# The front of a hybrid attention and pooling step, rebuilt without a transposed copy of x

## The chip, the cores and the metric

One NeuronCore of a Trainium2 chip runs the whole step. The metric is the device time of one execution in microseconds (us), as the median of some runs.

## What is computed

One layer works on 1024 prompt tokens and 8 sequences of 16 new tokens, 1152 tokens of 1024 channels, in fp32. Each of the 9 sequences has a conditioning vector c that sets shift and scale. The part at issue is the front:

```python
def _front(x, c, pos, w_ada, b_ada, w_in):
    mod = jax.nn.silu(c) @ w_ada + b_ada
    shift, scale, gate = jnp.split(mod, 3, axis=-1)
    h = (_layer_norm(x) * (1.0 + scale[:, None, :]) + shift[:, None, :])
    proj = h @ w_in
    q, k, v, g_attn, u, g_pool = jnp.split(proj, cuts, axis=-1)
    ...
```

Behind it come windowed attention with sinks (8 query heads, 2 key heads), a pooling mixer of four windows, SiLU gates, an output projection and a layer norm of alpha*x + gate*y.

## The kernel before

The kernel is written with an order by hand: each engine has its own program, and semaphores join them. An engine never passes a waiting instruction of its own.

**Units.** The input projection is cut into units: a block of 128 output columns (kinds k, v, ga, q, u, gp) for a chunk c of 384 tokens (chunks 0, 1, 2; chunk 2 has 256 prompt tokens and the 128 sample tokens). Units 0 to 5 are (k,0), (v,0), (k,1), (v,1), (k,2), (v,2). Products are made from a high and a low part, each operand as hi + lo with hi the value rounded to fp32r: per channel tile k (8 tiles of 128 channels) three matmuls, w_hi·h_hi, w_hi·h_lo, w_lo·h_hi, of 384 columns each, 24 a unit. Behind unit 5 the units 6 and up, attention slots among them, and the output projection fill TensorE's queue.

**The front.** SyncE loads x by tiles of 128 tokens (xs, a ring of XS = 6 tiles), the adaptive weights w_ada in six pieces of 512 columns (ada 0 to 3 shift and scale, in the order ADA = [0, 2, 1, 3, 4, 5], so that pieces 0 and 1 give shift and scale of channels 0 to 511; 4 and 5 the gate) and w_in by blocks. For each tile of x DVE makes statistics (x_stats, L969), GpSimd the inverse deviation (inv_std, L1260), ScalarE normalises in place (normalise, L786), TensorE transposes (x_transpose, L533, two halves of four channel tiles into the two PSUM banks of t_ps), and DVE and ScalarE copy these into xnT (evac_xt, L977 and L797), a copy of x with channels on partitions. For a piece of w_ada: ada (L505, TensorE, into s_ps), evac_ada (L790, ScalarE, into part), select (L525, TensorE, into o_ps), modulation (L981, DVE, into shT and s1T). Then h_ops (L992, DVE) applies scale and shift to xnT in place, h_high (L805, ScalarE) rounds to h_hi, and h_low (L1016 DVE, L1273 GpSimd) subtracts for h_lo, by pairs of channel tiles (H_ORDER). The samples of chunk 2 are modulated by h_samples (L1007). w_high (ScalarE) and w_low (DVE for blocks 0 and 1, GpSimd for the rest) do the same for w_in.

TensorE runs the first four units by halves (low: channel tiles 0 to 3; high: 4 to 7) with the transposes and the adaptive pieces between. Unit 3 has bank 0 of s_ps (EARLY), the others share three banks of proj_ps:

```python
            select(0)
            select(1)
            unit(0, low)
            x_transpose(3)
            unit(1, low)
            ...
            unit(3, low)
            for n in range(4):
                unit(n, high)
```

## Time and profile before

| | us |
|---|---|
| median of 3 runs | 462.62 |
| their range | 462.58 to 463.11 |
| the profiled execution | 464.38 |
| its span | 462.6 |
| TensorE matmul busy in the span | 429.2 (93%) |
| DVE busy | 285.5 (62%) |
| ScalarE busy | 129.9 (28%) |
| GpSimd busy | 118.4 (26%) |

PE is TensorE, DVE VectorE, ACT ScalarE, POOL GpSimd. The busy time of PE holds overlaps of pipelined matmuls, so it is not work at the peak rate. The mean granted clock of TensorE is 0.986 of full speed (2.4 GHz). In a row of a timeline, the bracket at the end is the idle time in front of the instruction and what ended it.

### The profile page before, as it was taken

How to read it: one execution, taken by the hardware profiler on the slowest of the kernel's cores; microseconds unless marked ns; L12 is line 12 of the kernel's file. 1: busy time of each engine (PE TensorE's matmuls, PEld its weight loads, DVE VectorE, ACT ScalarE, POOL GpSimd, SP SyncE). 2: the span in 40 equal slices, each digit the busy share in tenths (PEclk: the TensorE clock that was granted, in tenths of full speed). 3: DMA queues.
4: the chain of work that ended last, by engine and by line, in shares of the span. 5: the costliest groups of instructions: out<-in, count | busy, mean ns of one | idle time of the engine just before them, and what ended most of it. 6: DMA issues, size and time to landing. Idle time of an engine off the chain costs nothing.

```text
span 462.6 us, 6622 instructions
## 1 busy us (share of the span) xinstructions
PE 429.2 (93%) x2598; PEld 370.6 (80%) x2598; DVE 285.5 (62%) x541; ACT 129.9 (28%) x307; POOL 118.4 (26%) x83
## 2 busy tenths in 40 slices
...
GB/s 303 416 419 326 228 0 1 123 106 170 160 15 33 136 47 45 52 6 47 53 2 14 43 47 7 47 51 2 179 49 53 92 91 91 92 91 92 91 116 67
DMA packets 22545, 46.30 MB, mean 100 GB/s; under 512 B 11089, under 2 KB 13649, under 8 KB 21202
## 3 DMA queue, kind: packets, MB, share of 16 engines
...
q8 instruction: 21, 0.34, 0.3%
q14 instruction: 10, 0.08, 0.1%
...
## 4 chain that ended last, share of the span: by engine, by line
PE 78%; DVE 12%; ACT 4%; issue 3%; DMA 2%; POOL 1%; SPq 0%; DVEq 0%; POOLq 0%
PE proj_ps L585 14%; PE proj_ps L587 14%; PE proj_ps L586 14%; PE proj_ps L718 7%; PE proj_ps L720 7%; PE proj_ps L719 7%; PE t_ps L541 2%; PE s_ps L618 2%; PE t_ps L647 2%; PE s_ps L521 2%; DMA xs<-x_all 2%; DVE wo_lo L1143 2%; DVE xnT L1001 1%; ACT Pb L868 1%; PE proj_ps L561 1%
## 5 line engine op out<-in xcount | busy, mean ns | idle before, releaser
L585 PE MATMUL proj_ps<-h_hi,w_hi 128*128 128x384 f32 x400 | 139.2, 348 | 0.3 <-DVE rt L1036 0.3
L587 PE MATMUL proj_ps<-h_hi,w_lo 128*128 128x384 f32 x400 | 135.2, 338 | 0.0
L586 PE MATMUL proj_ps<-h_lo,w_hi 128*128 128x384 f32 x400 | 135.1, 338 | 0.0
L1271 POOL TENSOR_TENSOR w_lo<-w_raw,w_hi 128x1024 fp32r<-128x1024 f32 x16 | 41.4, 2585 | 154.1 <-ACT w_hi L814 154.1
L585 PEld LDWEIGHTS proj_ps<-h_hi,w_hi 128*128 128x128 f32 x400 | 75.8, 189 | 4.9 <-issue 2.2
L586 PEld LDWEIGHTS proj_ps<-h_lo,w_hi 128*128 128x128 f32 x400 | 75.8, 189 | 0.9
L587 PEld LDWEIGHTS proj_ps<-h_hi,w_lo 128*128 128x128 f32 x400 | 75.6, 189 | 0.0
L718 PE MATMUL proj_ps<-wo_hi,m_hi 128*128 128x512 f32 (+1 forms) x152 | 58.9, 387 | 4.4 <-DVE wo_lo L1143 3.8
L719 PE MATMUL proj_ps<-wo_lo,m_hi 128*128 128x512 f32 (+1 forms) x152 | 58.4, 384 | 0.0
L720 PE MATMUL proj_ps<-wo_hi,m_lo 128*128 128x512 f32 (+1 forms) x152 | 58.4, 384 | 0.0
L1058 DVE SCALAR_TENSOR_TENSOR mixed<-th,proj_ps 128x384 f32<-128x384 f32 x24 | 13.3, 553 | 56.5 <-ACT th L828 56.5
L718 PEld LDWEIGHTS proj_ps<-wo_hi,m_hi 128*128 128x128 f32 x152 | 28.6, 188 | 11.8 <-issue 4.3
L720 PEld LDWEIGHTS proj_ps<-wo_hi,m_lo 128*128 128x128 f32 x152 | 28.6, 188 | 6.2
L1263 POOL TENSOR_TENSOR rstd<-veps,mhalf 128x1 f32<-128x1 f32 x18 | 10.6, 589 | 89.8 <-DVE veps L967 89.8
L719 PEld LDWEIGHTS proj_ps<-wo_lo,m_hi 128*128 128x128 f32 x152 | 28.6, 188 | 6.0
L814 ACT ACTIVATE w_hi<-w_raw 128x1024 fp32r<-128x1024 f32 x18 | 18.9, 1057 | 38.3 <-PE proj_ps L587 33.9
L828 ACT ACTIVATE th<-proj_ps 128x384 f32<-128x384 f32 x24 | 11.8, 492 | 59.9 <-PE proj_ps L587 59.9
L868 ACT ACTIVATE Pb<-s_ps,negm 128x192 f32<-128x192 f32 (+3 forms) x72 | 28.1, 400 | 0.0
L881 ACT ACTIVATE m_hi<-mixed 128x1024 fp32r<-128x1024 f32 x9 | 9.5, 1059 | 62.5 <-PE proj_ps L720 61.7
L1246 DVE SCALAR_TENSOR_TENSOR yr<-yr,rstd,lnB 128x1024 f32<-128x1024 f32 (+1 forms) x10 | 25.8, 2590 | 0.3
L1136 DVE TENSOR_TENSOR den<-rs,es 128x4 f32<-128x4 f32 (+1 forms) x20 | 5.2, 259 | 33.5 <-ACT Pb L868 33.5
L1334 POOL TENSOR_TENSOR m_lo<-mixed,m_hi 128x1024 fp32r<-128x1024 f32 x8 | 23.5, 2935 | 4.1 <-ACT m_hi L881 4.1
...
## 6 DMA issues: line engine op xcount, KB each, us to landing
...
```

Of the source, the lines that this page charges most:

```text
L585: pe.matmul(bank[:, 0:CW], w_hi[:, w, k, :], hi, start=(k == 0), stop=False)
L586: pe.matmul(bank[:, 0:CW], w_hi[:, w, k, :], lo, start=False, stop=False)
L587: mm = pe.matmul(bank[:, 0:CW], w_lo[:, w, k, :], hi, start=False, stop=(k == KT - 1))
L718: pe.matmul(o, m_hi[:, t % 2, k, :], wo_hi[:, k, w], start=(k == 0), stop=False)
L719: pe.matmul(o, m_hi[:, t % 2, k, :], wo_lo[:, k, w], start=False, stop=False)
L720: mm = pe.matmul(o, m_lo[:, t % 2, k, :], wo_hi[:, k, w], start=False, stop=(k == KT - 1))
L814: act.activation(w_hi[:, b % 2], w_raw[:, b % RAW], ACT.Copy).then_inc(whi_done, 1)
L868: e = act.activation(Pb[:, i % 2, j, 0:nk], src, ACT.Exp, bias=negm[:, i % 2, j:j + 1], scale=SCALE, accum_out=rs[:, i % 2, j:j + 1])
L1058: dve.scalar_tensor_tensor(dst, th[:, i % 2, :], 1.0, src, ALU.add, ALU.mult).then_inc(dve_free, 1)
L1246: dve.scalar_tensor_tensor(r[:, w], r[:, w], rstd[:, TILES + t:TILES + t + 1], lnB[:, w], ALU.mult, ALU.add).then_inc(yb_done, 1)
L1271: pool.tensor_tensor(w_lo[:, b % 2], w_raw[:, b % RAW], w_hi[:, b % 2].bitcast(F32), ALU.subtract).then_inc(wlo_done, 1)
L1334: pool.tensor_tensor(m_lo[:, (t + 1) % 2], mixed[:, :, P * (t + 1):P * (t + 2)], m_hi[:, (t + 1) % 2].bitcast(F32), ALU.subtract).then_inc ...
```

## The change

xnT goes. xs now holds all nine tiles of x and lies where xnT lay (that room later takes mixed). The unit of work of the front is a channel tile of one chunk, listed in T_ORDER: first channel tiles 0 to 3 of chunks 0 and 1, then 4 and 5 of both, 6 and 7 of both, then chunk 2, where the samples come as two pieces ("s", four channel tiles each). TensorE transposes a channel tile of a chunk (three, two or for samples four transposes) into one of two banks of t_ps; DVE's h_full multiplies and adds from PSUM into a ring hx of HX = 5 places; ScalarE's h_high rounds hx into h_hi; GpSimd's h_low alone makes every low part of the prompt, and then the hx place is free. The bank of t_ps is free after h_full of it.

w_ada's columns are permuted on the host: piece a (0 to 3) holds shift and scale of the channel pair 2a, 2a+1. All four go through bank 1 of s_ps, so ada(a) waits until part a-1 is copied. Unit 2 has bank 0 of s_ps. x tiles 0 to 2 are loaded ahead of all adaptive weights, tiles 3 to 5 behind the first two pieces, 6 to 8 behind the last. TensorE's first six units run in pieces (first_unit), each with transposes of later tiles woven in. DVE makes w_lo of block 2 as well (DVE_LOW = 3).

```diff
-ADA = [0, 2, 1, 3, 4, 5]
-XS = 6
+HX = 5
...
+T_ORDER = [("p", c, k) for c in range(2) for k in range(4)] + [("p", c, k) for a in (4, 6) for c in range(2) for k in (a, a + 1)]
+T_ORDER += [("s", 2, 0)] + [("p", 2, k) for k in range(4)] + [("s", 2, 1)] + [("p", 2, k) for k in range(4, KT)]
+HI_ORDER = T_ORDER[:16] + [T_ORDER[m] for m in (17, 16, 18, 19, 20, 22, 21, 23, 24, 25)]
+LOW_ORDER = [x for x in T_ORDER if x[0] == "p"]
+SPARE_UNIT = 2
+BANK_BEFORE = {5: 3, 6: 0}
+DVE_LOW = 3
...
SyncE
-            load_ada(0)
             load_x(0)
+            load_x(1)
+            load_x(2)
...
-            load_ada(1)
+            load_ada(0)
             load_w(0)
             load_w(1)
+            load_ada(1)
             load_x(3)
             load_x(4)
             load_x(5)
+            load_ada(2)
+            load_ada(3)
             load_x(6)
             load_x(7)
             load_x(8)
...
-            sp.wait_ge(xt_done, 2 * TILES)
-            sp.dma_start(wada_late[:], w_ada[ADA[4]]).then_inc(ld_late, 16)
+            sp.wait_ge(ada_done, 4)
+            sp.dma_start(wada_late[:], w_ada[4]).then_inc(ld_late, 16)
...
TensorE
+            def x_transpose(*taus):
+                for tau in taus:
+                    kind, c, k = T_ORDER[tau]
+                    b = tau % 2
...
+                    if tau >= 2:
+                        pe.wait_ge(hx_done, tau - 1)
...
+            def first_unit(n, slices, taus=()):
...
+                for k in slices:
+                    if c == 2 and k % 4 == 0:
+                        pe.wait_ge(hhi_done, hi_count(("s", 2, k // 4)))
+                    pe.wait_ge(hhi_done, hi_count(("p", c, k)))
+                    pe.matmul(bank[:, 0:CW], w_hi[:, w, k, :], h_hi[:, k, cols(c)], start=(k == 0), stop=False)
+                    pe.matmul(bank[:, 0:CW], w_lo[:, w, k, :], h_hi[:, k, cols(c)], start=False, stop=False)
+                    if taus:
+                        x_transpose(taus.pop(0))
+                for k in slices:
+                    pe.wait_ge(hlo_p, LOW_ORDER.index(("p", c, k)) + 1)
...
+                    mm = pe.matmul(bank[:, 0:CW], w_hi[:, w, k, :], h_lo[:, k, cols(c)], start=False, stop=(k == KT - 1))
...
+            x_transpose(0, 1)
             ada(0)
...
             select(0)
+            first_unit(0, (0, 1), (2, 3))
+            first_unit(1, (0, 1))
+            ada(1)
             select(1)
+            first_unit(0, (2, 3))
+            first_unit(1, (2, 3))
             ada(2)
+            x_transpose(4, 5)
             select(2)
+            first_unit(2, (0, 1, 2, 3), (6, 7))
+            ada(3)
+            first_unit(3, (0, 1), (8, 9))
             select(3)
+            first_unit(3, (2, 3))
+            first_unit(0, (4, 5), (10,))
+            first_unit(1, (4, 5), (11,))
+            first_unit(2, (4, 5), (12,))
+            first_unit(3, (4, 5), (13,))
+            first_unit(0, (6, 7), (14,))
...
+            first_unit(3, (6, 7), (17,))
+            x_transpose(18)
+            first_unit(4, range(KT), range(19, len(T_ORDER)))
+            first_unit(5, range(KT))
...
ScalarE
             normalise(0)
+            normalise(1)
+            normalise(2)
             evac_ada(0)
             w_high(0)
+            h_high(0, 1)
             w_high(1)
             evac_ada(1)
+            h_high(2, 3)
             normalise(3)
             normalise(4)
             normalise(5)
+            evac_ada(2)
+            h_high(4, 5, 6, 7)
+            evac_ada(3)
             normalise(6)
+            h_high(8, 9)
             normalise(7)
+            h_high(10)
             normalise(8)
+            h_high(11, 12, 13, 14, 15)
...
DVE
+            def h_full(*taus):
...
+                    if i >= HX:
+                        dve.wait_ge(hlo_p, i - HX + 1)
+                    dve.wait_ge(mod_done, k // 2 + 1)
+                    dve.wait_ge(xt_done, tau + 1)
+                    dve.tensor_scalar(hx[:, i % HX, 0:pw], t_ps[:, b, 0:pw], s1T[:, k, 0:1], shT[:, k, 0:1], ALU.mult, ALU.add).then_inc(hx_done, 1)
...
+            modulation(0)
             w_low(0)
+            h_full(0, 1)
             w_low(1)
+            x_stats(3)
             modulation(1)
+            h_full(2, 3)
             x_stats(4)
             x_stats(5)
+            h_full(4)
+            modulation(2)
+            h_full(5, 6, 7)
```

Two places of TensorE's queue show the move. Before, the start of the queue holds the first adaptive pieces (L521), three tiles' transposes (L541) and both selections (L530) ahead of the first projection matmul (L576):

```order
L521 MATMUL s_ps<-wada_59,cpad 32x512 x8
L541 MATMUL t_ps<-ident,xs 128x128 x16
L521 MATMUL s_ps<-wada_60,cpad 32x512 x4
L541 MATMUL t_ps<-ident,xs 128x128 x8
L521 MATMUL s_ps<-wada_60,cpad 32x512 x4
L530 MATMUL o_ps<-sel,part 128x9 x8
L576 MATMUL proj_ps<-h_hi,w_hi 128x384
L577 MATMUL proj_ps<-h_hi,w_lo 128x384
```

Now (new lines: 562 transposes, 533 adaptive piece, 542 selection, 589 and 590 the high part's two matmuls, 597 the low part's):

```order
L562 MATMUL t_ps<-ident,xs 128x128 x3
L589 MATMUL proj_ps<-h_hi,w_hi 128x384
L590 MATMUL proj_ps<-h_hi,w_lo 128x384
L562 MATMUL t_ps<-ident,xs 128x128 x3
L597 MATMUL proj_ps<-h_lo,w_hi 128x384 x2
L589 MATMUL proj_ps<-h_hi,w_hi 128x384
L590 MATMUL proj_ps<-h_hi,w_lo 128x384
L589 MATMUL proj_ps<-h_hi,w_hi 128x384
L590 MATMUL proj_ps<-h_hi,w_lo 128x384
L597 MATMUL proj_ps<-h_lo,w_hi 128x384 x2
L533 MATMUL s_ps<-wada_59,cpad 32x512 x8
L542 MATMUL o_ps<-sel,part 128x9 x4
```

The second adaptive piece (wada_59 here, wada_60 before) and its selection, which stood ahead of the first projection matmul, now stand behind two channel tiles of unit 0 and of unit 1.

Unit 4 before is one run of matmuls with no transpose in it:

```order
L577 MATMUL proj_ps<-h_hi,w_lo 128x384
L576 MATMUL proj_ps<-h_hi,w_hi 128x384
L577 MATMUL proj_ps<-h_hi,w_lo 128x384
L576 MATMUL proj_ps<-h_hi,w_hi 128x384
L577 MATMUL proj_ps<-h_hi,w_lo 128x384
L576 MATMUL proj_ps<-h_hi,w_hi 128x384
L577 MATMUL proj_ps<-h_hi,w_lo 128x384
L581 MATMUL proj_ps<-h_lo,w_hi 128x384 x8
L585 MATMUL proj_ps<-h_hi,w_hi 128x384
```

Now, from its fifth channel tile on (L562 is a transpose of the next tile):

```order
L562 MATMUL t_ps<-ident,xs 128x128 x2
L589 MATMUL proj_ps<-h_hi,w_hi 128x384
L590 MATMUL proj_ps<-h_hi,w_lo 128x384
L562 MATMUL t_ps<-ident,xs 128x128 x2
L589 MATMUL proj_ps<-h_hi,w_hi 128x384
L590 MATMUL proj_ps<-h_hi,w_lo 128x384
L562 MATMUL t_ps<-ident,xs 128x128 x2
L589 MATMUL proj_ps<-h_hi,w_hi 128x384
L590 MATMUL proj_ps<-h_hi,w_lo 128x384
L562 MATMUL t_ps<-ident,xs 128x128 x2
L589 MATMUL proj_ps<-h_hi,w_hi 128x384
L590 MATMUL proj_ps<-h_hi,w_lo 128x384
```

Each later pair of matmuls waits for hhi_done of a channel tile whose transposes stand directly ahead of it in the same queue.

## Rows read from the trace of the kernel before

**Rows 1.** Busy time by stretch: us, then each engine's busy us (instructions), clock, DMA, GB/s.

```profile
27.32:35.72 8.40, 8.00 (x34) 7.46 (x35) 8.12 (x23) 5.08 (x6) 5.26 (x9) 0.65 1.02 421
35.72:50.62 14.90, 14.56 (x113) 10.77 (x112) 10.21 (x25) 11.22 (x17) 2.09 (x6) 1.00 0.68 243
50.62:60.99 10.37, 8.74 (x50) 8.23 (x49) 10.20 (x17) 3.79 (x6) 4.34 (x3) 1.00 0.54 228
60.99:70.33 9.34, 5.09 (x26) 3.82 (x25) 9.13 (x13) 2.25 (x5) 3.29 (x2) 1.00 0.00 0
70.33:76.35 6.02, 6.02 (x26) 6.02 (x26) 4.25 (x7) 0.83 (x1) 2.44 (x1) 0.72 0.00 0
...
76.35:463.00 386.65, 373.35 (x2286) 327.50 (x2285) 229.73 (x412) 96.01 (x263) 98.47 (x55) 1.00 0.21 69
```

**Rows 2.** TensorE's timeline at the start: start us, us, line, instruction, idle before.

```profile
9.08 1.93 PE L521 MATMUL s_ps<-wada,cpad 128*32 128x512 f32 x8 [0.50 <-DMA wada<-w_ada]
14.50 3.94 PE L541 MATMUL t_ps<-ident,xs 128*128 128x128 f32 x16 [3.49 <-ACT xs L788]
...
19.94 1.09 PE L541 MATMUL t_ps<-ident,xs 128*128 128x128 f32 x8
...
24.12 1.04 PE L530 MATMUL o_ps<-sel,part 128*128 128x9 f32 x8 [1.10 <-ACT part L795]
...
27.78 0.52 PE L577 MATMUL proj_ps<-h_hi,w_lo 128*128 128x384 f32 x1
28.10 0.52 PE L576 MATMUL proj_ps<-h_hi,w_hi 128*128 128x384 f32 x1
```

**Rows 3.** TensorE's timeline later in the front.

```profile
33.64 0.34 PE L586 MATMUL proj_ps<-h_lo,w_hi 128*128 128x384 f32 x1
33.81 0.34 PE L587 MATMUL proj_ps<-h_hi,w_lo 128*128 128x384 f32 x1
...
64.72 0.44 PE L576 MATMUL proj_ps<-h_hi,w_hi 128*128 128x384 f32 x1 [2.17 <-ACT h_hi L808]
...
68.51 1.49 PE L581 MATMUL proj_ps<-h_lo,w_hi 128*128 128x384 f32 x6 [1.75 <-DVE h_lo L1020]
...
71.10 0.53 PE L585 MATMUL proj_ps<-h_hi,w_hi 128*128 128x384 f32 x1
```

**Rows 4.** GpSimd's and DVE's timeline at 64.7 us and at 250.5 us.

```profile
64.74 1.84 POOL L1277 TENSOR_TENSOR h_lo<-xnT,h_hi 128x768 fp32r<-128x768 f32 x1 [2.31 <-ACT h_hi L808]
...
64.76 2.24 DVE L1038 TENSOR_TENSOR rt<-rt,sinT 128x384 f32<-128x384 f32 x1
...
250.46 2.57 POOL L1271 TENSOR_TENSOR w_lo<-w_raw,w_hi 128x1024 fp32r<-128x1024 f32 x1 [7.29 <-ACT w_hi L814]
...
250.73 0.56 DVE L1058 SCALAR_TENSOR_TENSOR mixed<-th,proj_ps 128x384 f32<-128x384 f32 x1
```

**Rows 5.** DVE's timeline: statistics of the first two tiles of x, and a modulation.

```profile
10.41 0.69 DVE L959 BATCH_NORM_STATS2 bnst<-xs 128x6 f32<-128x512 f32 x1 [6.70 <-DMA xs<-x_all]
...
12.11 0.69 DVE L959 BATCH_NORM_STATS2 bnst<-xs 128x6 f32<-128x512 f32 x1
...
25.19 0.20 DVE L989 SCALAR_TENSOR_TENSOR s1T<-o_ps,bT 128x36 f32<-128x36 f32 x1
```

**Rows 6.** Groups of DVE instructions: xcount, busy us, mean ns, idle before.

```profile
L1001 DVE TENSOR_SCALAR xnT<-xnT,s1T,shT 128x384 f32<-128x384 f32 x16 | 8.1, 570 | 1.2 <-ACT xnT L803 1.2
...
L975 DVE TENSOR_TENSOR w_lo<-w_raw,w_hi 128x1024 fp32r<-128x1024 f32 x2 | 2.4, 1220 | 1.3 <-ACT w_hi L814 1.3
...
L1116 DVE COPY PT<-t_ps 64x256 f32<-64x256 f32 x13 | 5.4, 415 | 4.0 <-PE t_ps L647 4.0
```

**Rows 7.** Groups of ScalarE instructions.

```profile
L788 ACT ACTIVATE xs<-xs,nmr,rstd 128x1024 f32<-128x1024 f32 x9 | 11.1, 1236 | 13.6 <-POOL nmr L1266 13.6
...
L795 ACT ACTIVATE part<-s_ps 128x512 f32<-128x512 f32 x6 | 3.6, 594 | 4.6 <-PE s_ps L521 4.6
...
L840 ACT ACTIVATE uext<-proj_ps 128x256 f32<-128x256 f32 x4 | 1.5, 385 | 14.5 <-PE proj_ps L587 14.5
```

More of the change, by code:

```diff
@@ L137, with hi_count @@
 SLOTS = {PLACES[4 * s // 3]: [s] for s in range(NSTEP + 2)}
[L141 to L149 removed]
+T_ORDER = [("p", c, k) for c in range(2) for k in range(4)] + [("p", c, k) for a in (4, 6) for c in range(2) for k in (a, a + 1)]
[5 more added lines that the diff above has]
+DVE_LOW = 3
+def hi_count(x):
+    return HI_ORDER.index(x) + 1
 def keys_of(i):
@@ L316, in hybrid_step @@
     ld_late = sem("ld_late")
-    ld_x = [sem(f"ld_x{i}") for i in range(XS)]
+    ld_x = [sem(f"ld_x{i}") for i in range(TILES)]
     ld_w = [sem(f"ld_w{i}") for i in range(RAW)]
@@ L557, in unit @@
+            def unit(n):
+                kind, j, c = UNITS[n]
+                bank = unit_bank(n)
+                wait_bank(n)
                 if kind == "z":
@@ L588, in unit @@
-                if slices[-1] == KT - 1:
-                    mm.then_inc(unit_done, 1)
-            def v_transposes(m):
-                pe.wait_ge(vte_done, m - 1) if m >= 2 else pe.wait_ge(xte_hi if m else xte_lo, TILES)
+                    if n == FIRST_UNIT[b]:
+                        weights_ready(b)
+                    for k in range(KT):
+                        hi, lo = h_hi[:, k, cols(c)], h_lo[:, k, cols(c)]
+                        pe.matmul(bank[:, 0:CW], w_hi[:, w, k, :], hi, start=(k == 0), stop=False)
+                        pe.matmul(bank[:, 0:CW], w_hi[:, w, k, :], lo, start=False, stop=False)
+                        mm = pe.matmul(bank[:, 0:CW], w_lo[:, w, k, :], hi, start=False, stop=(k == KT - 1))
@@ L1016, in h_low @@
-            def h_low(c, groups):
-                for g in groups:
-                    dve.wait_ge(hhi_done, H_ORDER.index((c, g)) + 1)
-                    w = slice(2 * g, 2 * g + 2)
-                    dve.tensor_tensor(h_lo[:, w, cols(c)], xnT[:, w, cols(c)], h_hi[:, w, cols(c)].bitcast(F32), ALU.subtract).then_inc(hlo_v, 1)
+                ks = slice(2 * a, 2 * a + 2)
+                sums = o_ps[:, 0:36].rearrange("p (k s) -> p k s", s=9)
+                for m, (dst, one) in enumerate(((shT, 0.0), (s1T, 1.0))):
+                    bias = bT[:, KT * m + 2 * a:KT * m + 2 * a + 2].unsqueeze(2).to_broadcast([P, 2, 9])
+                    last = dve.scalar_tensor_tensor(dst[:, ks, :], sums[:, 2 * m:2 * m + 2, :], one, bias, ALU.add, ALU.add)
@@ L1022, in evac_unit, with samples_low @@
+            def samples_low(half):
+                dve.wait_ge(hhi_done, hi_count(("s", 2, half)))
+                ks = slice(4 * half, 4 * half + 4)
+                dve.tensor_tensor(h_lo[:, ks, SEQ:TOK], hs[:, half], h_hi[:, ks, SEQ:TOK].bitcast(F32), ALU.subtract).then_inc(hlo_v, 1)
             def evac_unit(n):
@@ L1307, in _ @@
             inv_std(2)
-            h_low(0, (0,))
+            h_low(0, 1)
             inv_std(3)
+            h_low(2, 3)
             inv_std(4)
             inv_std(5)
+            h_low(4, 5, 6, 7)
             inv_std(6)
+            h_low(8)
             inv_std(7)
+            h_low(9)
             inv_std(8)
-            h_low(0, (2,))
-            h_low(1, (2,))
-            h_low(2, (0, 2))
-            for b in range(2, NBLK):
+            h_low(*range(10, len(LOW_ORDER)))
+            for b in range(DVE_LOW, NBLK):
                 s = (b - 12) // 2 if b < NBLK - 1 else 3
```

308 lines of the change are left out of this document (126 added, 182 removed).

## The prediction

> **What bounds the kernel now.** I read the busy times by stretch first, then TensorE's timeline at the start and where it stalls (a bracket there says what ended the idle time), then the price of each kind of front instruction on the other engines.
>
> The busy times by stretch [rows 1] show two kernels in one. From 76.35 us, where the sixth projection unit (v, chunk 2) is over, TensorE is busy 373.35 of 386.65 us at granted clock 1.00: the reader should see an engine that is the bound, whatever DVE, ScalarE and GpSimd do beside it. Ahead of it is the front, with 5.09 us busy of 9.34 in one stretch and a clock of 0.65 in another. What the front gains or loses at 76.35 us I take to reach the end one to one. The question is when unit 5 ends.
>
> TensorE's timeline at the start [rows 2] shows how differently one instruction costs: 16 transposes took 3.94 us at 14.50 (246 ns each), 8 took 1.09 us at 19.94 (130 ns), the two clock levels of 1.2 and 2.4 GHz. A 128x384 matmul starts every 0.32 us on the low level (27.78 to 28.10), every 0.17 us on the high one (33.64 to 33.81, [rows 3]; 0.174 over a whole unit). The clock was high at 24.12 and low at 27.78, after gaps of 1.10 us and some 2 us; it was low again at 71.10, after gaps of 2.17 and 1.75 us [rows 3].
>
> On DVE, an instruction with two SBUF operands stands still while GpSimd works: one of 384 columns took 2.24 us beside GpSimd's 1.84 us, and one of the same width that reads PSUM took 0.56 inside a GpSimd instruction of 2.57 us [rows 4].
>
> **The change, stretch by stretch.** I follow TensorE's queue from mark to mark. T is the transposition of one channel tile of a chunk (3 transposes, 2 in chunk 2, 4 for samples); DVE turns it into hx (h_full), ScalarE into h_hi, GpSimd into h_lo. Prices: h_full of 384 columns 0.56 [rows 4], of 256 0.42 [rows 6]; h_high 0.49 and 0.39, between 0.385 for 256 and 0.594 for 512 [rows 7]; h_low 0.95 and 0.66, half and a third of 1.84 for 768 [rows 4] with a little start-up. A hand-over between engines was 0.03 us (24.12 + 1.04 to 25.19, [rows 2, 5]); I allow 0.07.
>
> *1. To the first projection matmul: 27.3 us before [rows 1], 23.5 after.* Loads run at 421 GB/s [rows 1], and 2.1 MB of w_ada was there at 9.08 us [rows 2], so the flow starts at 4.0. Tile 0 of x now is ahead of the adaptive weights: statistics start at 5.6 us, not 10.41. Three tiles at 1.70 spacing [rows 5], 10.7; GpSimd some 1.2 with hand-overs (ScalarE's total wait says no more), 11.9; normalise(2) 1.24 [rows 7], 13.1. The adaptive piece 0 (3.8 MB in all) is there at 13.2. Then on the low clock: T0, T1 6 x 0.246 = 1.5, ada(0) 2 x 1.93 = 3.9 [rows 2], part 0.6, selection 1.9 (1.04 at the high level, [rows 2]), two modulations 0.3: 21.3. w_low(0), 1.22 [rows 6], stands ahead on DVE; h_full and h_high 1.1. **3.8 us gained.**
>
> *2. To the end of the first halves of units 0 and 1: 35.72 before, 39.8 after.* Before, channel tiles 0 to 3 have their modulations by 25.4 [rows 5]. Now ada(1) stands in TensorE's queue behind two pieces of units 0 and 1, and behind ada(1) the second modulation. From 23.5: 12 matmuls x 0.32 and 6 transposes x 0.246, 28.8; ada(1) 3.9; part 0.6, selection 1.8, modulations 0.35, h_full and h_high 1.2: 36.6 for the next projection matmul. GpSimd's two h_low 1.9, 38.5; then 7 matmuls at 0.174. I take the high level from 35 us on, since only then the queue is dense. 16.3 us for 8.4: **7.9 us lost**, 4.1 behind.
>
> *3. To the end of unit 3's first half: 50.62 before, 54.3 after.* ada(2) and ada(3) 2 x 1.9, two selections 1.8, 24 matmuls x 0.174 = 4.2, T4 to T9 18 x 0.13 = 2.3, waits 2.4: 0.5 for normalise(5), which ScalarE now does behind evac_ada(1), and 1.9 in unit 2, where T6 waits until h_full(5) has freed a PSUM bank. 14.5 for 14.9. **0.4 us gained**, 3.7 behind.
>
> *4. The four second halves: 60.99 before, 68.1 after.* Before, 10.37 us without a transpose. Now 48 x 0.174 = 8.4, T10 to T17 24 x 0.125 = 3.0, waits 2.4 (normalise(8), 1.24, stands on ScalarE between h_high of two tiles; the last h_low of a pair 0.4 four times). 13.8. **3.4 us lost**, 7.1 behind.
>
> *5. Unit 4 (k, chunk 2): 70.33 before, 81.5 after.* Before 9.34 us, of which 5.09 busy. Now T18 to T25 stand one behind each channel tile's pair of matmuls, and from the fifth tile on each pair needs the T issued directly ahead of it. The round trip is 0.1 (end of T) + 0.42 + 0.39 + three hand-overs 0.2 = 1.1 us of wait, at tiles 5, 6 and 7. At tile 4 the samples' T, two DVE instructions of 512 columns (0.69 each, as those of [rows 5]) and a copy of 0.59 [rows 7] lie in it: 2.4. Tiles 0 and 2: 1.3. Waits 7.0, work 24 x 0.174 + 18 x 0.125 = 6.4. 13.4 for 9.34. **4.1 us lost**, 11.2 behind.
>
> *6. Unit 5: 76.35 before, 85.8 after.* 24 x 0.174 = 4.2 for 6.02, since ten of the old ones ran on the low clock (0.72, [rows 1]). **1.8 us gained**, 9.4 behind. w_low(2), now DVE's, stands behind two rotations of k and ends by 84.7; unit 5 hides it. Without that cover it costs up to its 1.22.
>
> Sum: -3.8 + 7.9 - 0.4 + 3.4 + 4.1 - 1.8 = **+9.4 us**.
>
> At nothing I price the later w_in blocks, cosine and sine and wada_late: all the loads of the front are some 16 MB by their sizes in the program, there by 43 us at 421 GB/s, and their users come at 78 us or later; wada_late is asked for at ada(3)'s end, near 51 us, and used behind unit 7. If those 25 us went, its 2 MB, 5 us, would show.
>
> On gaps and the clock, rows and a rule part. The rows say that gaps of 2.17 and 1.75 us within a few us were enough to lower it. The Trainium skill, "TensorE: Matmul & The Clock Gate", section "Why this matters for your kernels", asks only for gaps of no more than about 3 us; by it the clock would stay high from about 20 us on in the new front, and part 2 would take 3.5 us less, +6 in all. I go by the rows.
>
> The change also moves DVE's modulation from SBUF to PSUM. The old instruction of 384 columns took 0.57 us in the mean, standstills included [rows 6], the new one is priced at 0.56: nothing gained. The Trainium skill, "GPSIMD Engine Reference", section "Key points", names as contending with GpSimd only DVE instructions with two SBUF inputs or in a two-port mode; the row of 0.56 us inside 2.57 agrees.
>
> **Rivals.**
> *The clock stays high (chance 0.20).* For: no gap of more than 2.8 us in TensorE's new order. Against: the falls at 27.78 and 71.10. Matmuls, transposes, ada(1) and selection of part 2 up to 35 us then cost half: 3.5 us less, +6, 468.6 us; with part 1 on the high level as well another 3 less, 465.6.
> *The clock falls in unit 4 too (0.20).* Unit 4 would be busy 6.4 of 13.4 us, a smaller share than the 5.09 of 9.34 behind which it was low at 71.10. Its last 16 matmuls and unit 5's 24 on the low level: 40 x 0.15 = 6 us at most; half of it is likelier, +12.5, 475.1.
> *Faster: the round trips hide (0.08).* If DVE, ScalarE and GpSimd run ahead of TensorE, so that of the waits 2.4 + 2.4 + 7.0 none is left, unit 5 ends at 85.8 - 11.8 = 74.0, 2.3 us earlier: 460.3. For it: the first matmul is 3.8 us earlier, and DVE's standstills go. It decides where TensorE's work between a T and its user is longer than 1.1 us; in unit 4 there is none, which speaks against.
> *GpSimd becomes the bound (0.05).* All low parts of the prompt go to it, 16 x 0.95 + 8 x 0.66 = 20.5 us; from 57 us on 14 of 24 remain, 11 us of work in the 23 before unit 4's end. 0.3 more for each would still be hidden; at twice the price it would add 4: 476.
> Within 0.2%: 0.02, by chance.
>
> **The numbers.** The profiled execution has 464.38 us with a span of 462.6, 1.8 around it; it is 1.8 above the median of 462.62. The sum is made in the span, and I add it to the median: 462.6 + 9.4 = 472.0. This case (0.45) runs from 470 to 474; with the clock's two rivals the range is 465.6 to 477. What can be told from no change is 0.2%, 0.9 us. Faster 0.08, same 0.02, slower 0.90.
>
> **What would show it.** First projection matmul at 22 to 24 us; the second modulation at 33 to 36 us, the largest loss; in unit 4 gaps of over 1 us at its last tiles, released by ScalarE's h_hi; unit 5 over near 86; from there 386 us. If the second modulation is there before 30 us, or unit 4 takes less than 9, the sum is wrong; if the rest behind unit 5 is not 386 us, the step one to one is.

## The result, and the profile after

| | before | changed |
|---|---|---|
| median of 4 runs, us | 462.65 (462.58 to 463.11) | 478.25 (477.08 to 479.05) |
| ratio | 1 | 1.032, interval 1.030 to 1.034 |
| profiled execution, us (span) | 464.38 (462.6) | 478.75 (477.0) |
| granted clock over the span | 0.986 | 0.971 |

The kernel is 15.6 us slower by the medians. By the two spans it is 14.4 us; the profiled execution of before was itself 1.8 above its median, that of the changed kernel 0.5. The forecast was 472.0 us in a range of 465.6 to 477: the sign is right, the time is 1.25 us outside the range.

The marks of TensorE's queue, each read from its timeline, beside the forecast ones (us; the last column is what each piece came to minus what was forecast for it):

| mark | before | forecast | changed | forecast missed by |
|---|---|---|---|---|
| 1, first projection matmul | 27.3 | 23.5 | 20.9 | -2.6 |
| 2, end of first halves of units 0 and 1 | 35.7 | 39.8 | 36.2 | -1.0 |
| 3, end of unit 3's first half | 50.6 | 54.3 | 52.6 | +1.9 |
| 4, end of the four second halves | 61.0 | 68.1 | 67.6 | +1.2 |
| 5, end of unit 4 | 70.3 | 81.5 | 85.5 | +4.5 |
| 6, end of unit 5 | 76.35 | 85.8 | 90.55 | +0.9 |
| to the end | 386.25 more | as before | 386.45 more | +0.2 |

The view of busy times by stretch, with the changed kernel's own marks (length; then PE, PEld, DVE, ACT, POOL busy with instructions; clock; DMA; GB/s):

```profile
20.89:36.16 15.27, 12.52 (x54) 8.93 (x54) 8.01 (x20) 5.78 (x8) 6.12 (x10) 0.72 1.02 417
36.16:52.57 16.41, 15.01 (x92) 8.96 (x91) 7.08 (x18) 5.73 (x9) 6.00 (x8) 0.89 0.65 238
52.57:67.55 14.98, 13.10 (x74) 10.63 (x73) 7.89 (x17) 6.20 (x10) 8.31 (x11) 1.00 0.29 120
67.55:85.46 17.91, 10.31 (x44) 8.22 (x42) 10.47 (x21) 4.73 (x11) 6.04 (x8) 0.77 0.00 0
85.46:90.55 5.09, 5.09 (x26) 5.09 (x25) 3.85 (x7) 1.06 (x1) 0.00 (x0) 0.80 0.02 3
90.55:477.00 386.45, 373.53 (x2287) 327.66 (x2286) 229.83 (x412) 96.01 (x263) 98.51 (x55) 1.00 0.22 69
```

Against [rows 1]: from unit 6 on, next to nothing has moved (386.45 us, clock 1.00 in both). The last stretch of [rows 1] runs to 463.00, 0.4 us past the end of the span of 462.6, so what it and the prediction call 386.65 is 386.25. The whole loss stands ahead of 90.55 us, and over half of it in the fourth line, unit 4: 17.91 us where before it was 9.34. PE is busy 10.3 us there, DVE 10.5 and ScalarE 4.7. No engine is the bound; they wait for each other. The fifth line has no idle time at all but a clock of 0.80: 5.09 us for work that takes 4.16 on the high level (73.48 to 77.64 in the first experiment's timeline below).

TensorE's timeline at the start, changed kernel, as [rows 2] and [rows 3] for before (start us, length us, instruction, count, idle before it and what ended it):

```profile
17.11 1.06 PE L542 MATMUL o_ps<-sel,part 128*128 128x9 f32 x8 [0.73 <-ACT part L836]
20.89 0.66 PE L589 MATMUL proj_ps<-h_hi,w_hi 128*128 128x384 f32 x1 [2.72 <-ACT h_hi L849]
...
26.18 1.92 PE L533 MATMUL s_ps<-wada,cpad 128*32 128x512 f32 x16
28.82 1.06 PE L542 MATMUL o_ps<-sel,part 128*128 128x9 f32 x8 [0.72 <-ACT part L836]
31.50 0.44 PE L589 MATMUL proj_ps<-h_hi,w_hi 128*128 128x384 f32 x1 [1.62 <-ACT h_hi L849]
...
34.11 0.52 PE L589 MATMUL proj_ps<-h_hi,w_hi 128*128 128x384 f32 x1
34.43 0.52 PE L590 MATMUL proj_ps<-h_hi,w_lo 128*128 128x384 f32 x1
...
36.16 3.64 PE L533 MATMUL s_ps<-wada,cpad 128*32 128x512 f32 x16
```

The reader should see the two costs of the new order. Behind the first two selections the next matmul waits 2.72 and 1.62 us, a whole trip through DVE and ScalarE. And from the first projection matmul on the clock changes its level three times: the matmuls up to 26.18 us are 0.32 us apart, the low level; ada(1) takes 1.92 us for 16, the high one; those at 34.11 and 34.43 are 0.32 apart again, and ada(2) at 36.16 takes 3.57 us until the next instruction at 39.73, from where on it is high.

The same view in unit 4:

```profile
70.93 0.44 PE L589 MATMUL proj_ps<-h_hi,w_hi 128*128 128x384 f32 x1 [0.62 <-ACT h_hi L849]
...
74.99 0.44 PE L589 MATMUL proj_ps<-h_hi,w_hi 128*128 128x384 f32 x1 [2.43 <-ACT h_hi L844]
75.27 0.34 PE L590 MATMUL proj_ps<-h_hi,w_lo 128*128 128x384 f32 x1
75.44 0.38 PE L562 MATMUL t_ps<-ident,xs 128*128 128x128 f32 x2
77.01 0.53 PE L589 MATMUL proj_ps<-h_hi,w_hi 128*128 128x384 f32 x1 [1.19 <-ACT h_hi L849]
...
77.66 0.63 PE L562 MATMUL t_ps<-ident,xs 128*128 128x128 f32 x2
79.47 0.69 PE L589 MATMUL proj_ps<-h_hi,w_hi 128*128 128x384 f32 x1 [1.19 <-ACT h_hi L849]
...
82.09 0.69 PE L589 MATMUL proj_ps<-h_hi,w_hi 128*128 128x384 f32 x1 [1.18 <-ACT h_hi L849]
...
82.90 2.76 PE L597 MATMUL proj_ps<-h_lo,w_hi 128*128 128x384 f32 x8
85.46 0.52 PE L589 MATMUL proj_ps<-h_hi,w_hi 128*128 128x384 f32 x1
```

Each tile from 74.99 on has the same figure: two matmuls, T (the transposition of a channel tile), 1.19 us of nothing, the next. At the high level one round is 77.01 - 74.99 = 2.02 us, then 2.46 and 2.62. From there on the clock is low: T takes 0.63 (77.66) in place of 0.38 (75.44), and the eight last matmuls take 2.56 us where they would take 1.39. One round trip in DVE's and ScalarE's timelines:

```profile
75.96 0.54 DVE L1045 TENSOR_SCALAR hx<-t_ps,s1T,shT 128x256 f32<-128x256 f32 x1 [2.00 <-PE t_ps L562]
```

```profile
76.54 0.42 ACT L849 ACTIVATE h_hi<-hx 128x256 fp32r<-128x256 f32 x1 [1.60 <-DVE hx L1045]
```

T ends at 75.44 + 0.38 = 75.82. DVE has its result by 76.50, ScalarE from 76.54 to 76.96, the matmul starts at 77.01: 0.14 + 0.54 + 0.04 + 0.42 + 0.05 = 1.19.

### The profile page after: what moved, and what is told of

It reads as the page before. It is cut to its first block, busy times and chain, and to the rows that moved or that the text cites. A ratio compares the mean times of both kernels' runs of the same rounds, so it can differ in the third digit from the quotient of the medians.

```text
span 477.0 us, 6715 instructions
## 1 busy us (share of the span) xinstructions
PE 435.8 (91%) x2598; PEld 372.2 (78%) x2598; DVE 277.0 (58%) x535; ACT 126.9 (27%) x309; POOL 127.4 (27%) x101
## 4 chain that ended last, share of the span: by engine, by line
PE 79%; DVE 11%; ACT 4%; issue 2%; DMA 1%; POOL 1%; SPq 0%; DVEq 0%; POOLq 0%
PE proj_ps L620 13%; PE proj_ps L621 13%; PE proj_ps L622 13%; PE proj_ps L756 6%; PE proj_ps L758 6%; PE proj_ps L757 6%; PE s_ps L533 3%; PE s_ps L656 2%; PE t_ps L685 2%; DVE hx L1045 2%; PE proj_ps L589 2%; DVE wo_lo L1172 2%; PE proj_ps L597 1%; ACT Pb L909 1%; ACT h_hi L849 1%
## 5 line engine op out<-in xcount | busy, mean ns | idle before, releaser
L620 PE MATMUL proj_ps<-h_hi,w_hi 128*128 128x384 f32 x384 | 132.9, 346 | 0.0
L622 PE MATMUL proj_ps<-h_hi,w_lo 128*128 128x384 f32 x384 | 129.1, 336 | 0.0
L621 PE MATMUL proj_ps<-h_lo,w_hi 128*128 128x384 f32 x384 | 129.1, 336 | 0.0
L1293 POOL TENSOR_TENSOR w_lo<-w_raw,w_hi 128x1024 fp32r<-128x1024 f32 x15 | 38.9, 2594 | 154.5 <-ACT w_hi L855 154.5
L620 PEld LDWEIGHTS proj_ps<-h_hi,w_hi 128*128 128x128 f32 x384 | 72.2, 188 | 4.2 <-issue 2.2
L621 PEld LDWEIGHTS proj_ps<-h_lo,w_hi 128*128 128x128 f32 x384 | 72.2, 188 | 0.9
L622 PEld LDWEIGHTS proj_ps<-h_hi,w_lo 128*128 128x128 f32 x384 | 72.2, 188 | 0.0
L1303 POOL TENSOR_TENSOR h_lo<-hx,h_hi 128x384 fp32r<-128x384 f32 (+1 forms) x24 | 22.1, 924 | 41.4 <-ACT h_hi L849 25.1
L589 PE MATMUL proj_ps<-h_hi,w_hi 128*128 128x384 f32 x40 | 17.8, 446 | 12.0 <-ACT h_hi L849 8.5
L1045 DVE TENSOR_SCALAR hx<-t_ps,s1T,shT 128x384 f32<-128x384 f32 (+1 forms) x24 | 15.0, 631 | 22.3 <-PE t_ps L562 21.9
```

The source lines that it names most:

```text
L589: pe.matmul(bank[:, 0:CW], w_hi[:, w, k, :], h_hi[:, k, cols(c)], start=(k == 0), stop=False)
L620: pe.matmul(bank[:, 0:CW], w_hi[:, w, k, :], hi, start=(k == 0), stop=False)
L621: pe.matmul(bank[:, 0:CW], w_hi[:, w, k, :], lo, start=False, stop=False)
L622: mm = pe.matmul(bank[:, 0:CW], w_lo[:, w, k, :], hi, start=False, stop=(k == KT - 1))
L1045: dve.tensor_scalar(hx[:, i % HX, 0:pw], t_ps[:, b, 0:pw], s1T[:, k, 0:1], shT[:, k, 0:1], ALU.mult, ALU.add).then_inc(hx_done, 1)
L1293: pool.tensor_tensor(w_lo[:, b % 2], w_raw[:, b % RAW], w_hi[:, b % 2].bitcast(F32), ALU.subtract).then_inc(wlo_done, 1)
```

## The experiments

All edits are made to the changed kernel unless another is named. "Before" in a batch is the kernel before, run on the same chip between the others: 463.38 us in the first batch, 463.61 in the second, 463.31 in the third; ratios are to it, and are what is compared between batches (they are taken over the runs of a batch and can differ by 0.001 from the quotient of the two medians). The changed kernel was not run again in these batches: its ratio, 1.032, is that of the first table.

**Is it the round trips of unit 4?** Transposes 10 to 25 are put two to each of the eight second-half pieces, whose matmuls use older tiles, and unit 4 is left with none. The same instructions, in another order. ScalarE's order follows.

```diff
-            first_unit(0, (4, 5), (10,))
-            first_unit(1, (4, 5), (11,))
+            first_unit(0, (4, 5), (10, 11))
+            first_unit(1, (4, 5), (12, 13))
...
-            x_transpose(18)
-            first_unit(4, range(KT), range(19, len(T_ORDER)))
+            first_unit(3, (6, 7), (24, 25))
+            first_unit(4, range(KT))
```

> The changed kernel, but the transposes of chunk 2 (T18 to T25) are issued two at a time inside the eight second-half pieces of units 0 to 3, so that none is left inside unit 4. Theory A (the loss sits in unit 4's round trips, T directly ahead of its user, and in the low clock that they bring): unit 4 takes 4.2 to 4.5 us instead of 17.9, unit 5 4.2 instead of 5.1, the second halves about 1 us more; in all 12 to 14 us less than the changed kernel, 464 to 466 us. Rival B (GpSimd, which now makes all 24 low parts of the prompt, is the bound): its work of 1.0 us for 384 and 0.73 for 256 columns is the same, it waits less, but unit 4 only moves by what GpSimd runs ahead: no more than 3 us less, 475 or above. Rival C (shape of the start: the second adaptive piece in the queue): no change, 478.

Measured: 465.15 us (464.8 to 465.88), ratio 1.0037, interval 1.0022 to 1.0052. TensorE's timeline of this kernel:

```profile
62.68 0.44 PE L562 MATMUL t_ps<-ident,xs 128*128 128x128 f32 x2 [0.84 <-DVE hx L1043]
...
69.33 0.34 PE L589 MATMUL proj_ps<-h_hi,w_hi 128*128 128x384 f32 x1
...
72.10 1.55 PE L597 MATMUL proj_ps<-h_lo,w_hi 128*128 128x384 f32 x8
73.48 0.34 PE L589 MATMUL proj_ps<-h_hi,w_hi 128*128 128x384 f32 x1
...
77.64 0.34 PE L620 MATMUL proj_ps<-h_hi,w_hi 128*128 128x384 f32 x1
```

The stretch of the second halves in this kernel (columns as above):

```profile
52.74:69.33 16.59, 14.73 (x92) 12.29 (x92) 13.62 (x26) 9.40 (x18) 12.53 (x16) 1.00 0.26 108
```

Unit 4 goes from 69.33 to 73.48 without a wait, unit 5 to 77.64. The second halves take 16.59 us for the changed kernel's 14.98, since they now hold 18 transposes more. Their waits are no longer: three, for DVE to free a PSUM bank (0.84, 0.64, 0.25, together 1.7), in place of the five of the changed kernel (1.8). No matmul waits for h_hi there any more. Unit 4 then ends 12.0 us earlier. The weave takes back 13 of the 15.6 us. Theory A holds, for round trips and clock together; the next experiment parts them. GpSimd takes no less time for its 24 subtractions (22.8 us in all, for 22.0 in the changed kernel), so it was not the bound, and rival B falls; so does rival C, since the start is as it was.

**How much of unit 4 is the clock?** Five extra matmuls, whose result nothing uses, stand behind each of the last four transposes, where TensorE would be idle.

```diff
+                    if n == 4 and 3 <= k <= 6:
+                        for m in range(5):
+                            pe.matmul(s_ps[:, 1, 0:CW], w_hi[:, w, 0, :], h_hi[:, 0, cols(0)], start=True, stop=True)
```

> The changed kernel with five extra 384-column matmuls into an unused PSUM bank behind each of the transposes T22 to T25 inside unit 4; they compute nothing that is used and fill the waits of 1.2 us (5 x 0.174 = 0.87 us at the high clock). Theory A with the clock as its second half: the clock no longer falls at 77 us, tiles 5 to 7 take 2.0 us each instead of 2.6, the eight low matmuls 1.4 instead of 2.6, unit 5 4.2 instead of 5.1: 3 to 4 us less, 474 to 475.5. If gaps alone count and the clock costs nothing (rival D), the extra matmuls change nothing or cost up to 1 us: 478 to 479.

Measured: 474.94 us (473.68 to 475.5), ratio 1.0244, interval 1.0221 to 1.0268; the changed kernel's is 1.032, so 3.5 us less. Its TensorE timeline in unit 4:

```profile
74.34 0.44 PE L589 MATMUL proj_ps<-h_hi,w_hi 128*128 128x384 f32 x1 [1.55 <-ACT h_hi L847]
...
74.93 1.12 PE L595 MATMUL s_ps<-h_hi,w_hi 128*128 128x384 f32 x5
76.36 0.44 PE L589 MATMUL proj_ps<-h_hi,w_hi 128*128 128x384 f32 x1 [0.31 <-ACT h_hi L852]
...
80.40 0.44 PE L589 MATMUL proj_ps<-h_hi,w_hi 128*128 128x384 f32 x1 [0.31 <-ACT h_hi L852]
...
80.85 1.55 PE L600 MATMUL proj_ps<-h_lo,w_hi 128*128 128x384 f32 x8
82.24 0.34 PE L589 MATMUL proj_ps<-h_hi,w_hi 128*128 128x384 f32 x1
```

Its unit 4 as a stretch (clock 1.00, for 0.77 in the changed kernel):

```profile
66.91:82.24 15.33, 11.24 (x64) 9.29 (x63) 8.98 (x19) 4.72 (x11) 6.08 (x8) 1.00 0.00 1
```

Every round is now 2.02 us (74.34, 76.36, then 78.38 and 80.40), the eight last matmuls 1.39 (80.85 to 82.24), unit 5 4.16. The waits for h_hi, 0.31, are what the fill leaves of 1.19. So TensorE did more work and ended sooner, as the theory expected, and rival D falls. The clock's share is 2.6 us in unit 4 (15.33 for 17.91) and 0.9 in unit 5. Of the 13.1 us that the weave took back, 9.6 are then left for the round trips: most of them are the waits of the changed kernel's unit 4, 7.6 us, and 1.3 us of work that is slower around these.

**The place of the second adaptive product.** ada(1) and select(1) ahead of unit 1's first pieces.

```diff
             first_unit(0, (0, 1), (2, 3))
-            first_unit(1, (0, 1))
             ada(1)
             select(1)
+            first_unit(1, (0, 1))
```

> The changed kernel with one piece moved: ada(1) and select(1) ahead of unit 1's first piece on TensorE, so the second modulation does not wait for that piece. The data of ada(1) should be there by 20.5 us. Theory A says the second modulation comes 2 us earlier (28 instead of 29.9) and the mark at ada(2) 1.5 to 2.5 us earlier than 36.2; but the rest is a matter of round trips, so the end comes 0.5 to 2 us earlier, 476 to 478. Rival C (the loss is made at the start, in the order of the adaptive pieces): at least 4 us earlier, 474 or less.

Measured: 475.66 us (473.99 to 477.52), ratio 1.0263, interval 1.0226 to 1.03: some 2.6 us less, a little more than expected, and not the 4 of rival C. The wait behind select(1) falls from 1.62 to 0.48 us, and ada(2) runs at the high level (1.86 us, for 3.57). The profiled execution is the slowest of the four, and the recorded marks don't hold in it: the second selection ends at 30.4 us where the second modulation was expected at 28, and ada(2) starts 0.6 us earlier, not 1.5 to 2.5. In it 1.2 us were given away at the start (first projection matmul at 22.06, for 20.89, behind a selection at the low level, 1.88 us). At the end of unit 3's first half it is 2.3 us ahead (50.26), and in unit 4 it loses 1.3 of them again (19.25 us for 17.91), the clock being low from 68.9 us until unit 5. So the split between order and clock isn't settled by it.

**The load order at the start, both ways.** First, the changed kernel with the old load order:

```diff
+            load_ada(0)
             load_x(0)
-            load_x(1)
-            load_x(2)
...
-            load_ada(0)
+            load_x(1)
+            load_x(2)
```

> The changed kernel with the loads in the old order at the start: both halves of adaptive piece 0 ahead of x tile 0, and tiles 1 and 2 behind the small tables. First transposes then at about 14.5 us instead of 8.8, and the first projection matmul 3 to 5 us later than 20.9. Theory A: the whole queue moves back by this, 3 to 5 us more, 481 to 483, since ada(1) is behind the same instructions. If the end is set by what comes later (the loads of x tiles 3 to 8 or the adaptive pieces 2 and 3, rival E), the end hardly moves: within 1 us of 478.

Measured: 482.76 us (481.95 to 484.52), ratio 1.0421, interval 1.0396 to 1.0445. T0 is at 14.50 us in place of 8.76 and the first projection matmul at 26.88 for 20.89; some of these 6.0 are got back behind, where ada(2) takes 2.14 us for the changed kernel's 3.57. Theory A holds (481 to 483 expected). The new load order is worth 4.7 us to this kernel. Then the kernel before with the new load order:

```diff
-            load_ada(0)
             load_x(0)
+            load_x(1)
+            load_x(2)
...
-            load_x(1)
-            load_x(2)
+            load_ada(0)
```

> The kernel before with the change's load order alone: x tiles 0 to 2, the identity, the selection rows and the bias ahead of the two first adaptive weight tiles. Theory A (the load order is of use only to a kernel whose transposes come before the adaptive product; here the product still gates the modulation and the first matmul): 0 to 2 us less than the kernel before, 461 to 463. Rival F (the load order alone gives what it gave the change, 4.5 us): 458 to 459. Rival G (the product comes later, since its weights are behind the x tiles on the queue): 463.5 to 467.

Measured: 463.03 us (461.75 to 464.43), ratio 0.9991, interval 0.9978 to 1.0003: no change that can be told. Its first projection matmul is at 27.53 us, for 27.3 before. It reached the second selection 0.6 us earlier (23.52 for 24.12), and that selection then took 1.85 us, on the low level, for 1.04. The load order is worth something only to the new order of TensorE's queue: in the kernel before the first projection matmul waits for two adaptive products and the 24 transposes of three tiles of x, whichever data comes first. What the new queue order would be worth at the start without the load order was not parted from the rest.

**The price of h_full.** The shift is a constant (the line is shortened here).

```diff
-dve.tensor_scalar(hx[...], t_ps[...], s1T[:, k, 0:1], shT[:, k, 0:1], ALU.mult, ALU.add)
+dve.tensor_scalar(hx[...], t_ps[...], s1T[:, k, 0:1], 0.25, ALU.mult, ALU.add)
```

> The change with the prompt's shift replaced by the constant 0.25 in h_full: it leaves out the shift of the modulation, the number of instructions is the same. Theory P (each per-partition scalar read through a pointer costs the vector engine some 0.06 us an instruction): h_full takes 0.61 to 0.62 us for 384 tokens and 0.48 for 256 in place of 0.68 and 0.54, and the round trips of unit 4 are 0.06 us shorter each. Rival Q (it is the read from PSUM with the modulation's arithmetic that costs it): 0.68 and 0.54 unchanged. The whole time: 477 to 479 either way.

The groups of DVE instructions in the changed kernel, and then in this one (columns as in [rows 6]):

```profile
L1045 DVE TENSOR_SCALAR hx<-t_ps,s1T,shT 128x384 f32<-128x384 f32 x16 | 10.6, 674 | 15.5 <-PE t_ps L562 15.1 <-POOL h_lo L1303 0.4
...
L1045 DVE TENSOR_SCALAR hx<-t_ps,s1T,shT 128x256 f32<-128x256 f32 x8 | 4.3, 543 | 6.8 <-PE t_ps L562 6.7
```

```profile
L1045 DVE TENSOR_SCALAR hx<-t_ps,s1T 128x384 f32<-128x384 f32 x16 | 9.7, 614 | 14.1 <-PE t_ps L562 13.7 <-POOL h_lo L1303 0.4
...
L1045 DVE TENSOR_SCALAR hx<-t_ps,s1T 128x256 f32<-128x256 f32 x8 | 3.9, 482 | 7.1 <-PE t_ps L562 7.0
```

0.674 falls to 0.614 for 384 columns and 0.543 to 0.482 for 256: 0.06 us for one per-partition scalar, at both widths. Theory P holds, and each wait of 1.19 in unit 4 is 1.12. Taking 0.06 more off for the second, which wasn't run, gives an estimate of 0.554 and 0.42, the 0.56 and 0.42 that the prediction had taken from instructions without such scalars. The whole time, one run, was 475.45 us, under the 477 to 479 expected. At the end of unit 5 it is 3.3 us ahead; 2.3 of them are there at 43.2 us already, and 1.7 of these are ada(2), 1.85 us for 3.57: from 36 to 40 us its clock was 1.00 and that of the changed kernel's profile 0.54. That part is the clock, not the scalar.

**Both orders at once.**

> Both orders at once: the transposes of round trips 10 to 25 two to each second-half piece, and ada(1), select(1) ahead of unit 1's first pieces. Theory A (the time above the kernel before lies in TensorE's waits for h_hi, and the two places are independent): the weave alone gave 465.15, the swap alone took some 2.6 off the change, of which the weave leaves what lies ahead of ada(2); 462.5 to 464. Rival B (the weave already gives the vector engine so much to do in the second halves that an earlier second modulation buys nothing): 464.8 to 465.8, the weave's own time. Rival C (earlier transposes pile onto GpSimd's h_lo queue): over 466.

Measured: 462.05 us (461.13 to 463.38, 12 runs), ratio 0.9966, interval 0.9955 to 0.9978. That is 0.0071 lower in the ratio than the weave alone, 3.3 us, more than the swap alone gave and a little more than theory A's 462.5 to 464; rivals B and C fall. It is the first version that beats the kernel before. Part of the 3.3 us is the clock: ada(2) took 1.86 us here and 3.57 in the weave's profile. Its TensorE timeline, and DVE's at the first modulation:

```profile
20.99 0.66 PE L589 MATMUL proj_ps<-h_hi,w_hi 128*128 128x384 f32 x1 [2.72 <-ACT h_hi L848]
...
24.46 2.79 PE L533 MATMUL s_ps<-wada,cpad 128*32 128x512 f32 x16
27.98 1.06 PE L542 MATMUL o_ps<-sel,part 128*128 128x9 f32 x8 [0.73 <-ACT part L835]
```

```profile
18.49 1.21 DVE L1008 TENSOR_TENSOR w_lo<-w_raw,w_hi 128x1024 fp32r<-128x1024 f32 x1
19.62 1.25 DVE L1043 TENSOR_SCALAR hx<-t_ps,s1T,shT 128x384 f32<-128x384 f32 x2
```

They show what is left: 2.72 us ahead of the first projection matmul, of which 1.2 is w_low(0), which stands on DVE between the modulation's sums and h_full(0), though DVE had been idle for 8.4 us ahead of them.

**Fill that wait.** Seven matmuls of the weight tile against itself behind select(0), on top of both orders.

```diff
             select(0)
+            pe.wait_ge(whi_done, 1)
+            for m in range(7):
+                pe.matmul(s_ps[:, 0, 0:CW], w_hi[:, 0, 0, :], w_hi[:, 0, 0:3, :], start=True, stop=True)
```

> As the kernel with both orders, and seven matmuls of 384 columns of the first high weight tile against itself, into the selected modulation's bank, behind select(0), where TensorE otherwise stands for some 2.7 us before the first projection matmul. Their results are used by nothing. Theory A with the clock: the granted clock stays at its upper level over the first pieces, and the first projection stage up to ada(2) is 1 to 3 us shorter than with both orders alone: 460 to 462.5. Rival D (the clock falls there for another reason than the idle stretch, or was up anyway): no change from both orders, within 0.5 us. Rival E (the extra matmuls hold the first projection matmul back): 0.5 to 1.5 us more.

Measured: 461.78 us (459.76 to 462.51, 7 runs), ratio 0.9949, interval 0.993 to 0.9968, which overlaps that of both orders. TensorE's timeline, and its busy time in one stretch (length, busy, clock, DMA, GB/s):

```profile
19.24 2.59 PE L767 MATMUL s_ps<-w_hi 128*128 128x384 f32 x7
22.11 0.66 PE L589 MATMUL proj_ps<-h_hi,w_hi 128*128 128x384 f32 x1 [0.28 <-ACT h_hi L851]
22.57 0.52 PE L590 MATMUL proj_ps<-h_hi,w_lo 128*128 128x384 f32 x1
```

```profile
20.90:23.90 3.00, 2.72 (x10) 1.00 1.05 421
```

The extra matmuls were themselves slow (0.37 us each) and held the first projection matmul back by 1.1 us (22.11 for 20.99), as rival E has it; ada(1) at 25.24 was back on the high level (1.92 for 2.79), and at select(1) both are level (27.88 and 27.98), as at ada(2) (34.09 and 34.20), where theory A had expected 1 to 3 us. The whole time didn't rise either, as rival E would have it. No gain that can be told. A puzzle stays open: matmuls at 22.11 and after are at the low pace, 0.32 us apart, where the recorded clock of the stretch is 1.00. In this stretch the record doesn't tell the pace.

**Take the wait away instead.** On top of both orders, the first weight tile is rounded while DVE and ScalarE are idle.

```diff
 ScalarE:
-            evac_ada(0)
             w_high(0)
+            evac_ada(0)
 DVE:
-            modulation(0)
             w_low(0)
+            modulation(0)
             h_full(0, 1)
```

> Both orders, and the rounding of the first projection weight tile (w_high(0) on ACT, w_low(0) on the vector engine) ahead of the first adaptive eviction and the first modulation, where both engines stand idle; in the kernel with both orders w_low(0) stands for 1.2 us between the modulation's sums and h_full(0). Theory A (this round trip ends the wait of TensorE before its first projection matmul): that matmul comes 1.0 us earlier, at 19.9 to 20.0, TensorE's wait there is 1.7 us in place of 2.7, and the time is 0.5 to 1.5 us less than with both orders alone, 460.5 to 461.5 beside the same kernel before. Rival H (the second adaptive product waits for its weights, so what is won ahead of it is lost there): the first matmul earlier and the time the same, within 0.4 us. Rival I (w_raw lands too late and ACT's queue holds the eviction back): the first matmul later, and 0.5 us more.

Measured: 460.56 us (460.04 to 461.09), ratio 0.9935, interval 0.9921 to 0.9949.

```profile
20.06 0.66 PE L589 MATMUL proj_ps<-h_hi,w_hi 128*128 128x384 f32 x1 [1.71 <-ACT h_hi L848]
...
23.27 1.92 PE L533 MATMUL s_ps<-wada,cpad 128*32 128x512 f32 x16
25.91 1.06 PE L542 MATMUL o_ps<-sel,part 128*128 128x9 f32 x8 [0.72 <-ACT part L835]
```

The wait is 1.71 us and the first projection matmul is at 20.06, 0.93 earlier. At select(1) the kernel is 2.07 us ahead (25.91 for 27.98), since ada(1) now runs on the high level (1.92 for 2.79). Theory A holds, and rivals H and I fall; this is the fastest kernel of the study, 3 us below the kernel before by its ratio (0.0065 x 463.3).

**The same edit to the changed kernel alone.**

> The change with the earlier rounding of the first weight tile alone. Theory A: the first projection matmul at 19.9, and 0.5 to 1.5 us less than the change, 476.5 to 477.8. Rival H: 478, the change's own time, since the second modulation's round trip and the stretch at the lower clock are left as they are.

Measured: 476.76 us (475.78 to 477.4), ratio 1.0278, interval 1.0256 to 1.0299, 1.9 us less than the changed kernel by the ratios, whose intervals don't quite touch.

```profile
17.51 1.88 PE L542 MATMUL o_ps<-sel,part 128*128 128x9 f32 x8 [0.72 <-ACT part L836]
21.11 0.66 PE L589 MATMUL proj_ps<-h_hi,w_hi 128*128 128x384 f32 x1 [1.71 <-ACT h_hi L849]
...
31.07 0.44 PE L589 MATMUL proj_ps<-h_hi,w_hi 128*128 128x384 f32 x1 [1.62 <-ACT h_hi L849]
```

The wait fell by 1.0 us, but select(0) ran at the low level here (1.88), so the first projection matmul was not earlier (21.11 for 20.89), and at 31.07 the kernel is 0.43 ahead. More came from ada(2), 1.85 us in place of 3.57. The time agrees with theory A, but its mark, the first projection matmul at 19.9, failed, and the marks don't decide between it and H. The two intervals are of different batches and lie 0.0001 apart, so the gain itself is barely shown.

## Why the prediction was wrong in size and right in sign

**Step 5, unit 4, is the step that failed: 13.4 us forecast, 17.9 measured.** Its mechanism, a round trip at every tile from the fifth on, was right, and the weave shows that it is where most of the loss lies. What was wrong was the size: the sum took all work of unit 4 at the high clock level, as dense work, with too short a round trip. Three terms, from the timelines above:
- The clock, +2.6: from 77.34 us on everything is at the low level. The rounds of 2.46 and 2.62 are 0.44 and 0.60 above 2.02, the last pair 0.36, the eight last matmuls 1.17.
- The price of the round trip, +0.6: the six forecast waits came to 7.6 us for 7.0. For one round 1.19 stands for 1.1, of which h_full is +0.12. The prediction took its price from DVE instructions without per-partition scalars. The trace of before had a warning which it didn't read: the instruction at L1063, 384 columns from PSUM with one per-partition scalar, took about 0.61 us, where L1058, without one, took 0.56 [rows 4].
- The stops, +1.3, which is what the other two leave: TensorE's work was forecast at its dense rate, 0.174 a matmul and 0.125 a transpose. Behind a wait the matmul lets the next one start only 0.28 us later (74.99 to 75.27), and a T of two with a wait behind it counts its whole 0.38 us, for the 0.25 of the forecast. That is 0.23 for each of the six waits.

**The rival "the clock falls in unit 4 too" came true**, at 3.5 us with unit 5 (its guess was 3, its bound 6). It had a chance of 0.20. The row at 71.10 [rows 3] spoke for it, low behind gaps of 2.17 and 1.75 us, and it should have been the main case. With it the forecast would have been 475.1, and the measured time still 3 above.

**Step 6, +0.9**, is the same fall: six matmuls of unit 5 on the low level. w_low(2) was hidden, as forecast.

**Step 1, -2.6.** Statistics began at 4.58 us, not 5.6; the adaptive product took 3.2 and not 3.9, and the selection 1.06 and not 1.9, since the clock was back on the high level by 17 us. Some of this is luck: in the swap's profile, whose order is the same up to there, the two took 3.64 and 1.88, and the first projection matmul came at 22.06. The form of the step was right: 2.72 us of wait, with w_low(0) in it, as the experiment that takes it out shows.

**Step 2, -1.0, is two errors that nearly cancel.** The first pieces took the 5.3 us forecast at the low level. ada(1) ran at the high level (1.92 for 3.9), and the next projection matmul came 31.50 - 26.18 = 5.3 us behind its start where 7.8 were forecast. But behind the wait of 1.62 us after select(1) the low level was back (clock 0.50 from 33.6 to 36.2), and the matmuls forecast at 0.174 took 0.32. The second modulation, expected at 33 to 36 us, was over at 30.2, which the prediction had itself named as a sign that its sum is wrong.

**Step 3, +1.9**, is again that fall: ada(2) took 3.57 for 1.9, where the prediction had taken the high level from 35 us on. The waits of unit 2 were 1.3 us for the 2.4 priced. The other 1.3 is work above the dense rate, which wasn't taken apart here.

**Step 4, +1.2.** The five waits were 1.8 us, not 2.4, and four of them are GpSimd's last h_low of a pair, as forecast. (The prediction's own terms, 1.24 and four times 0.4, make 2.8; its sum has 2.4.) The work was 13.2 and not 11.4, and the timeline says where:

```profile
53.92 0.33 PE L597 MATMUL proj_ps<-h_lo,w_hi 128*128 128x384 f32 x1
54.62 0.44 PE L597 MATMUL proj_ps<-h_lo,w_hi 128*128 128x384 f32 x1 [0.37 <-POOL h_lo L1303]
```

The four pieces that stop for h_lo take 0.44 to 0.54 us each above the dense rate, their waits not counted, and the four that don't stop take 0.02 to 0.05 less than it. The matmul ahead of a wait counts 0.33 in place of 0.174, the one behind it 0.28. A transposition with no stop costs nothing extra: a T of three lets the next matmul start after 0.25 us, and that one takes 0.26, together 0.51 for the 0.55 priced. So the price is one of stops, not of transpositions.

**One to one held**: 386.45 us behind unit 5, for 386.25. **The faster rival fell**: the round trips are not hidden, since in unit 4 each tile's user stands right behind it; where the order gives them cover, as in the weave, they nearly are. **GpSimd as the bound fell**: its instructions took 1.00 and 0.73 us for the 0.95 and 0.66 priced, and TensorE waited for h_lo five times, 0.34 to 0.41 us each.

The sum of the misses is 4.9 us in the span, to rounding; the other 1.3 of the 6.2 is that the forecast was added to the median and the profiled execution of before was 1.8 above it, the changed one 0.5.

On the rule weighed in the prediction: behind the changed kernel's gaps of 2.43 and 1.19 us the granted clock was 0.50 (79.5 to 87.3 us), and it had been 0.50 behind gaps of 0.72 and 1.62 (33.6 to 36.2). The Trainium skill, "TensorE: Matmul & The Clock Gate", section "Why this matters for your kernels", asks for no idle gaps over about 3 us; the trace doesn't agree that this is enough, since none behind the first transposition, at 8.76 us, was that long (the longest was 2.72).

Beside GpSimd's instructions h_full, which reads PSUM, was never longer than its usual 0.68 us for 384 columns; w_low(1), with two SBUF inputs, took 1.63 us beside them, for the 1.22 of w_low(0) without. The Trainium skill, "GPSIMD Engine Reference", section "Key points", names as contending only DVE instructions with two SBUF inputs or in a two-port mode, and the trace agrees.
